# A two-block model kernel: feed-forward norms moved behind the products, and products, residuals and sums kept in PSUM

## The reference, cut to what matters

```python
def rms_norm_2(x, g):
    xf = x.astype(jnp.float32)
    y = xf * lax.rsqrt(jnp.mean(xf * xf, axis=-1, keepdims=True) + RMS_EPS)
    return (y * g.astype(jnp.float32)).astype(x.dtype)

def swiglu(h, w_gate, w_up, w_down):
    return (jax.nn.silu(h @ w_gate) * (h @ w_up)) @ w_down
...
        n = rms_norm_2(h, ffn1_norm[l])
        h = h + 0.5 * swiglu(n, ffn1_w_gate[l], ffn1_w_up[l], ffn1_w_down[l])
```

## Time and profile before

| | |
|---|---|
| three runs | 1078.06, 1083.63, 1083.65 us, median 1083.63 |
| the profiled execution | 1077.73 us |
| its span, first to last instruction | 1075.9 us |
| busy share: PE, POOL, ACT, DVE | 92%, 61%, 50%, 50% |
| mean granted clock of TensorE | 0.974 of full speed |

### The profile page before, as it was taken

How to read it: one execution, slowest core, us unless ns; L and a number is a source line. 1 busy time by engine, 2 the same in 40 slices (tenths; PEclk the granted TensorE clock), 3 DMA queues, 4 the chain that set the end, 5 groups by cost and what they waited for, 6 DMA issues and landing times.

```text
span 1075.9 us, 22914 instructions
## 1 busy us (share of the span) xinstructions
PE 992.6 (92%) x9068; PEld 944.6 (88%) x9068; DVE 533.0 (50%) x735; ACT 535.2 (50%) x765; POOL 654.8 (61%) x271
## 2 busy tenths in 40 slices
PE   5998999799799778999999999999999999999996
PEld 5987777698799767899999998999898879999996
DVE  4346424654410895586662003375274668777301
ACT  6565564556554445644444436676331554444441
POOL 2785234356689731698787775554620269888882
PEclk9998999999899899999999999999899999999999
DMA  8553122133355200455555553333300046555551
GB/s 321 195 169 106 60 79 98 59 118 128 127 177 177 79 1 2 149 187 177 177 171 177 176 176 124 117 117 115 99 4 4 23 136 207 188 192 179 192 177 41
DMA packets 38993, 139.79 MB, mean 130 GB/s; under 512 B 4224, under 2 KB 5504, under 8 KB 38784
## 3 DMA queue, kind: packets, MB, share of 16 engines
q1 hardware_dynamic: 38912, 138.62, 38.7%
HBM read 137.55 MB, written 1.05 MB: 129 GB/s over the span
## 4 chain that ended last, share of the span: by engine, by line
PE 55%; issue 21%; POOL 12%; DVE 8%; ACT 2%; DMA 1%; SPq 0%; POOLq 0%; DVEq 0%; ACTq 0%
PE ps L667 55%; POOL wlo L602 11%; DVE qkl L1834 3%; DVE hA L2133 1%; DVE hT L1866 1%; ACT whi L1463 1%; ACT dif L1402 1%; DMA ring<-in_stream 1%; DVE sq L1834 0%; ACT rstd L1402 0%; POOL dif L626 0%; PE ps L1208 0%; DVE hA L1834 0%; DVE rGI L1834 0%; DVE aL L1872 0%
## 5 line engine op out<-in xcount | busy, mean ns | idle before, releaser
L602 POOL TENSOR_TENSOR wlo<-ring,whi 128x1024 fp32r<-128x1024 f32 x251 | 611.8, 2455 | 372.4 <-ACT whi L1463 371.5
L667 PE MATMUL ps<-aH,whi 128*128 128x256 f32 (+1 forms) x1528 | 444.0, 291 | 27.5 <-DVE aL L1834 11.8
L667 PE MATMUL ps<-aH,wlo 128*128 128x256 f32 (+1 forms) x1528 | 438.2, 287 | 0.0
L667 PE MATMUL ps<-aL,whi 128*128 128x256 f32 (+1 forms) x1528 | 437.8, 287 | 0.0
L1463 ACT ACTIVATE whi<-ring 128x1024 fp32r<-128x1024 f32 x253 | 266.3, 1058 | 122.9 <-PE ps L667 107.3
L667 PEld LDWEIGHTS ps<-aH,whi 128*128 128x128 f32 x1528 | 293.4, 192 | 35.3 <-POOL wlo L602 17.6
L667 PEld LDWEIGHTS ps<-aL,whi 128*128 128x128 f32 x1528 | 292.8, 192 | 0.5 <-issue 0.4
L667 PEld LDWEIGHTS ps<-aH,wlo 128*128 128x128 f32 x1528 | 293.1, 192 | 0.0
L667 PE MATMUL ps<-fH,wlo 128*128 128x272 f32 (+1 forms) x352 | 100.8, 286 | 0.0
L667 PE MATMUL ps<-fH,whi 128*128 128x272 f32 (+1 forms) x352 | 100.4, 285 | 0.0
L667 PE MATMUL ps<-fL,whi 128*128 128x272 f32 (+1 forms) x352 | 100.4, 285 | 0.0
(11 more groups left out here) (336 smaller groups left out, 1279.0 us busy)
## 6 DMA issues: line engine op xcount, KB each, us to landing
ring<-in_stream SPq DMA_DIRECT2D x253, 512.0 KB, 3.3
cst<-in_cst SPq DMA_DIRECT2D x1, 1325.0 KB, 13.1
xT<-in_x SPq DMA_DIRECT2D x4, 272.0 KB, 3.7
out<-hT SPq DMA_DIRECT2D x1, 1024.0 KB, 4.6
row<-in_row SPq DMA_DIRECT2D x1, 898.0 KB, 9.7
cst<-in_cst SPq DMA_DIRECT2D x1, 640.0 KB, 10.6
mat<-in_mat SPq DMA_DIRECT2D x1, 576.0 KB, 14.0
vec<-in_vec SPq DMA_DIRECT2D x1, 135.0 KB, 3.8
```

Source lines behind the costliest of these rows:

```text
L602: nc.gpsimd.tensor_tensor(wlo[:, s, :], ring[:, s, :], whi[:, s, :].bitcast(F32), ALU.subtract).then_inc(S("w_split"), 1)
L667: return nc.tensor.matmul(out, lhsT, rhs, start=start, stop=stop, skip_group_check=True)
```

## The change

- **Late norms.** The two feed-forward layers take `x * w`, split into `fxH` and `fxL` behind each residual tile, and `rstd` is multiplied in later: on the gate product ahead of tanh, and on the down product in the next `residual`. PE runs the first pair of units ahead of the sum over the squares, and does no `filler` there. The meta tokens' part is made in the HGRN layer (`meta_high`, `meta_low`).
- **PSUM.** The product `fact` stays in the PSUM bank of the up product till it is split; for the feed-forward layers the new residual is made in PSUM (`late_tile`) and copied to `xT`; the running sums of squares are in PSUM (`sq_sum`), and `norm0`, `ffn1`, `ffn2` sum seven of eight squares on DVE.
- **Attention split early.** `mixT` tiles 4 to 7 are split at steps 31 and 32 of `even_in`, into `fxH`/`fxL` (the memory of `hT` and `mixT`).
- **RWKV.** `inverse_starts` stands ahead of the low parts of units `U_PO` and on, which now also wait for `r_u`; the turns of the keys stand ahead of and between the products of `r_u`.
- **Start and end.** In the first norm the second unit's high and low parts come after `rstd`, and the output goes out in four transfers of two tiles.

```diff
-SUMMED = 5
+LATE = ("ffn1", "ffn2")
+SUMMED = {"norm0": 7, "norm1": 5, "ffn1": 7, "mix": 5, "ffn2": 7, "final": 5}
...
-            sp.wait_ge(S("norm_h"), len(NORMS) * KT)
-            sp.dma_start(out_d, hT[:, :, TM:TT]).then_inc(S("out_done"), 16)
+            for k in range(0, KT, 2):
+                sp.wait_ge(S("norm_h"), (len(NORMS) - 1) * KT + k + 2)
+                sp.dma_start(out_d[:, k:k + 2, :], hT[:, k:k + 2, TM:TT]).then_inc(S("out_done"), 16)
...
-            lows(U_HO + SLOTS, U_PO + SLOTS)
+            lows(U_HO + SLOTS, U_PO)
             inverse_starts()
-            lows(U_PO + SLOTS, N_UNITS)
+            pool.wait_ge(S("r_u"), 3)
+            lows(U_PO, N_UNITS)
...
-                feature_pair(u0, g0, c0, ("norm_h", NORMS.index(tag) * KT))
+                feature_pair(u0, g0, c0, ("norm_h", NORMS.index(tag) * KT), tag)
+                norm(tag, TT - c0)
...
                 def gate(it, f4):
-                    act.wait_ge(S("w_used"), it * 8 + (u0 + 2 * f4 + 1))
+                    ahead(u0 + 2 * f4, it)
+                    act.wait_ge(S("ffn_gate"), it * 4 + (first + f4 + 1))
...
-                    ahead(u0 + 2 * f4, it)
                     ahead(u0 + 2 * f4 + 1, it)
...
+                    if j == 31:
+                        act.wait_ge(S("att_o"), 8)
+                        for n in range(4):
+                            func(fxH[:, 4 + n, TM:TT], mixT[:, 4 + n, TM:TT], ACT.Copy, "mix_hi")
...
+                        if tag in ("mix", "final"):
+                            tt(out, out, rstd[:, 0:TT - c0], ALU.mult)
+                        if tag in LATE:
+                            stt(late_tile(m), out, scale, xT[:, m, c0:TT], ALU.mult, ALU.add, "drained_v")
+                            step(nc.vector.tensor_copy(xT[:, m, c0:TT], late_tile(m)), "resid_x")
...
-                    half, prod = fhalf[:, c0:TT], fact[:, f4 % 2, c0:TT]
+                    half, prod = fhalf[:, c0:TT], ps[:, (g0 + 2 * f4 + 1) % MM_BANKS, 0:TT - c0]
+                    gate = ps[:, (g0 + 2 * f4) % MM_BANKS, 0:TT - c0]
+                    dve.wait_ge(S("w_used"), it * 8 + (u0 + 2 * f4 + 1))
+                    nc.vector.tensor_tensor(gate, gate, rstd[:, 0:TT - c0], ALU.mult).then_inc(S("ffn_gate"), 1)
```

169 lines of the change are left out of this document (107 added, 62 removed).

## The result

| | before | after |
|---|---|---|
| runs | 1078.06, 1083.63, 1083.65, 1084.77 us | 1051.78, 1052.63, 1053.72, 1054.47 us |
| median | 1083.64 us | 1053.18 us |
| the profiled execution | 1077.73 us | 1053.72 us |
| its span | 1075.9 us | 1051.9 us |
| mean granted clock | 0.974 | 0.980 |

The changed kernel takes 0.9726 of the time of before, with a 95% interval of 0.9699 to 0.9753. The predicted 1053 us and its range hold. But the sum said 26.6 us against the profiled execution, the two traces differ by 24.0, and the medians by 30.5; and of the things named as signs of an error two came. So the terms have to be looked at one by one.

What follows compares the result with a forecast made beforehand. PE, busy 992.6 of 1075.9 us, bounds the kernel; only its waits and lower-clock places count. Eight gains sum to 26.6, taking the profiled 1077.7 to 1051.1; the median was put at 1053, range 1043 to 1067.

Steps and rivals of the forecast that it cites:

- Start: First norm: PE starts earlier as weight work moves behind rstd; 1.3 us gained, between 0 and 1.4.
- Norm ahead of HGRN: Sums of squares in PSUM end DVE's arrears, so the norm falls from 8.82 to 5.70 us: 3.1, from 1.5 to 3.3.
- Even output product: Even layer's output product: early attention split removes PE's 7.52 us wait and slow start; 4.0 gained, from 1.0 to 5.8.
- First feed-forward norm: Ahead of the first feed-forward layer: the 5.70 us gap closes, two sum products added; 4.7 gained, 3.7 to 5.7.
- RWKV, fills first: RWKV masks: POOL's earlier fills remove PE's 2.44 us wait and the lower clock behind it; 5.2 gained, from below 2.4.
- free, and so are the SP transfers that wait for them: RWKV: POOL's low parts moved behind `r_u`, and the weight transfers waiting for them, cost nothing.
- Turns of keys: RWKV: earlier turns remove PE's wait for DVE's copies (1.52 of 3.69 us); 1.4 gained, from 0 to 1.5.
- Second feed-forward norm: Ahead of the second feed-forward layer: the gap of 8.01 us shrinks; 6.0 gained, between 4.0 and 7.0.
- rival (a): PE's new starts meet late low weights or the lower clock, giving half the gain back: 1064 to 1069 us; chance 0.14.
- Output: Final transfer: output sent in pieces, so the last quarter saves 0.9 us, from 0 to 2.
- Rival (b): DVE operations with one PSUM and one SBUF operand are held up by POOL too: 1059 to 1065 us; chance 0.06.
- Rival (c): Feed-forward loop: chain gate product, DVE scaling, ACT tanh, `fhalf` sets the pace; slower, 1086 at 0.8 a pair; chance 0.04.

Runs made afterwards that it cites:

- the run without the wait: Changed kernel with ACT's heads' square moved behind the even layer's last drain and a high part, another high part ahead of the tanh: 1050.2 us.
- The experiment: Changed kernel with, ahead of the second feed-forward layer, one table load left out and weights' high parts ahead of the squares: 1052.2 us.

## Why the prediction was right, and where it wasn't

The bound was read rightly: PE's waits at named places and nothing inside the feed-forward stretch (200.0 of 200 us busy before, 199.1 after). The start, the first feed-forward norm and the output have no run of their own; what is said of them rests on the two traces. Term by term:

- **Start** (1.3): 1.1. PE starts 1.7 us earlier (14.20 for 15.89), of which 1.1 are left at 62 us.
- **Norm ahead of HGRN** (3.1): 3.3. With the sums in PSUM, 432 ns each, PE waits for no square. With the sums back in SBUF 1.7 of it is lost.
- **Even output product** (4.0): 2.8, inside the bounds. The split did leave the path. For falling to the lower clock "in this wait" I gave 1.6; the run without the wait shows 2.7 against the changed kernel's trace and 1.7 to 1.9 against five others with the same waits. So the sum was near what mostly happens, and 0.8 to 1.0 of the 1.2 missing here is a longer cold stretch in the one trace. The cost of POOL's low part beside the big product (up to 1.3) was 2.1 (3.32 for 1.23).
- **First feed-forward norm** (4.7): 4.8. PE begins the pair with a wait of 0.30 for low weights and none for `fxH` or `fxL`.
- **RWKV, fills first** (5.2): 6.0 in the traces. The wait and the lower clock behind it were seen; undone in the changed kernel the fills cost 7.6, as the cold stretch isn't of one length.
- "free, and so are the SP transfers that wait for them": **wrong**. The order moved four transfers from PE's long matmuls to its densest stretch of short ones, back to back, and PE lost 1.4 there (1.2 to 2.2 in the seven profiles with this order). I looked at who waits for the low parts and not at what runs beside the transfers.
- **Turns of keys** (1.4): right as a wait, and shown net as 0.0 for the reason above. What I had not seen is that this wait decides before's usual level: 4.3 us more in the one profile taken at that level, and the run with the turns moved leaves that level in six of seven runs. "Which of the two levels the new median takes I can't tell" has an answer: the changed kernel doesn't have that level's cause. That the predicted median of 1053 came out is luck: two errors cancelled, 2.6 too much in the sum against 2 added for a level that is gone.
- **Second feed-forward norm** (6.0): 4.6. The step that failed is that this term holds no wait for low weights, where the first norm's lower end had one: as rival (a) said, PE's pair met a late low part (1.99, with 0.42 behind), since ACT waits for DVE's tiles with a high part queued behind. The experiment gave 1.3 of it back; the DVE backlog I had counted with stood right behind it.
- **Output** (0.9): 2.2, and all of it is the transfer (4.6 us to landing before, 2.4 now). Pieces of 256 KB land in 2.4 us and not in the 3.7 of the input's pieces; these start together at the very beginning, and were no row for it.
- **Unforeseen**: -1.9 and +1.5. Of the first, 1.6 is a stretch at the lower clock (176 to 180 us, 0.57) that no other profile here has, though the wait of 1.2 us ahead of it is in all of them; the other 0.3 comes with the early split. The second is a cold stretch that before had at 668 to 672 us. It isn't the chance of one trace: all three profiles of before and of before with the turns moved have it, and of the eleven of the changed kernel and its versions only one. So it may belong to the change, but nothing here shows by what, for the rows ahead of it wait the same 0.39 in both. The -0.4 in the HGRN layer wasn't followed up.

Rival (b), that operations with one operand in PSUM are held too, fell: `fL` 425 ns and sums 432 on average, while with all operands in SBUF the sums take 951 on average and `fL` 2.41 us in the loop. The rule of the Trainium skill (SBUF — State Buffer, section Who interferes with whom), by which an operation of DVE with at most one input in SBUF and outside the two-port modes doesn't contend with GpSimd, while with two such inputs or in a two-port mode the one that issues second is blocked till the first has ended, agrees with all of these. The Trainium skill's other figures (Perfetto Trace Analysis, section Optimizing Scalar/DVE Operations), about 60 ns of overhead for DVE on SBUF and about 125 on PSUM, some 65 more by my estimate, aren't borne out here: 424 ns for the copy out of PSUM (before's trace has 419 for a subtraction in SBUF of the same 256 elements), and one and the same operation, `fxL`, takes 484 ns reading PSUM and 0.48 us reading SBUF with no low part beside it.

Rival (c) was rightly small for this change, but my reason for it (the pair's chain leaves 3 us) holds only because `fact` went to PSUM in the same change. I had booked that as "nothing gained". In the sum it is worth nothing; taken out of the changed kernel it costs 51 us.

Of the signs named in advance, the clock of 0.50 behind 226 us and the wait for `wlo` at the second start came, in the places where the sum is 1.2 and 1.4 too high; the others didn't.

Open: why TensorE falls to the lower clock behind a wait in one run and not in the next (62 to 66 us in four of the profiles, 176 to 180 in one, behind the wait of 1.99 for the second feed-forward layer's low weights in two, each about 1.5 us, with the same waits ahead of them to 0.05 us), why it stays there longer in one run than in the next (224 to 232 us), what removed the stretch at 668 us, and by what the transfers hold PE.

## What to carry to other kernels

A wait of 1.5 us on the bounding engine can cost nearly 6 (5.6 here): price it with the cold stretch that may follow, and look at the spread of the runs, since two levels are a sign of such a wait. One trace gives the price of a cold stretch only to about 1 us, so look at the same place in every profile that shares the code. When a helper operation is moved, move its transfer in mind too, and look at what stands beside it at the new place. A part of a change that gains nothing by the profile of before can be what makes another part possible: count an engine's round with the new operations in it, in series, at the durations that they have when the neighbour's operations come in step.
